# GLA and SSD layer: the attention's gate and V as merged units with tokens on the partitions

## The reference

```python
h = rms_norm(x, pre_norm_w) * (1 + scale) + shift
q, k, v, g, gate_lr, z, xbc, dt_raw = split(h @ w_in)        # GLA head: dk = 128, dv = 256
log_a = log_sigmoid(gate_lr @ gla_gate_w2 + gla_gate_b) / 16
b = cumsum(log_a) in the chunk
q_dec, k_dec, k_end = q * exp(b), k * exp(-b), k * exp(b_last - b)
o = tril(q_dec k_dec^T) v + q_dec S;   S = S * exp(b_last) + k_end^T v
o = rms_norm(o, gla_norm_w)          # over the head's 256 values of a token
o = o * silu(g)
...
out = concat(o, y) @ w_out;  x + gate * rms_norm(out, post_norm_w)
```

## Time and profile before

| what | value |
|---|---|
| median of 3 runs | 1676.37 us (1673.08 to 1678.06) |
| the profiled execution | 1671.3 us, of which span 1669.6 us |
| TensorE busy | 1610.1 us, 96% of the span |
| VectorE / ScalarE / GpSimd busy | 1049.6 / 840.7 / 397.1 us (63% / 50% / 24%) |
| mean granted clock of TensorE | 0.992 of full speed |
| DMA | 231.14 MB, mean 138 GB/s |

### The profile page before, as it was taken

How to read it: one execution, slowest core, us unless ns; L and a number is a source line. 1 busy time by engine, 2 the same in 40 slices (tenths; PEclk the granted TensorE clock), 3 DMA queues, 4 the chain that set the end, 5 groups by cost and what they waited for, 6 DMA issues and landing times. The chain is left out here.

```text
span 1669.6 us, 27425 instructions
## 1 busy us (share of the span) xinstructions
PE 1610.1 (96%) x9990; PEld 1385.7 (83%) x9990; DVE 1049.6 (63%) x1754; ACT 840.7 (50%) x1496; POOL 397.1 (24%) x449
## 2 busy tenths in 40 slices
PE   5999999999999999998999999999999999999997
PEld 4888888888888888888888887888888878888886
DVE  5545454465444554456777777877777754885986
ACT  5755554545544554464454555655455554334332
POOL 2311000101322222200223222223323220451523
PEclk9999999999999999999999999999999999999999
DMA  9523442265434533334222225322212326765886
GB/s 327 139 90 113 143 125 61 83 186 146 159 126 134 188 120 128 124 109 145 74 74 76 73 77 152 113 94 91 77 70 74 113 101 206 244 237 165 314 266 199
DMA packets 131358, 231.14 MB, mean 138 GB/s; under 512 B 9907, under 2 KB 81859, under 8 KB 126134
## 3 DMA queue, kind: packets, MB, share of 16 engines
q1 hardware_dynamic: 123910, 190.76, 35.6%
q10 hardware_dynamic: 6512, 38.80, 6.3%
q0 software_dynamic: 832, 0.22, 0.4%
HBM read 177.05 MB, written 52.70 MB: 138 GB/s over the span
## 5 line engine op out<-in xcount | busy, mean ns | idle before, releaser
L1155 PE MATMUL ps<-hl,w 128*128 128x512 f32 x1488 | 372.9, 399 | 0.1
L1155 PEld LDWEIGHTS ps<-hl,w 128*128 128x128 f32 x1488 | 273.9, 188 | 56.4 <-issue 1.4
L1875 PE MATMUL ps<-hl,w 128*128 128x256 f32 x2304 | 293.6, 287 | 0.0
L1875 PEld LDWEIGHTS ps<-hl,w 128*128 128x128 f32 x2304 | 281.1, 192 | 7.9 <-issue 7.9
L1161 PE MATMUL ps<-w,hl 128*128 128x256 f32 x1536 | 200.6, 287 | 0.0
L1161 PEld LDWEIGHTS ps<-w,hl 128*128 128x128 f32 x1536 | 190.5, 191 | 2.4
L1741 DVE SCALAR_TENSOR_TENSOR c_acc<-c_before,conv_col,c_acc 128x256 f32<-128x256 f32 x288 | 158.3, 551 | 47.2 <-ACT c_acc L1609 40.3
L1879 PE MATMUL ps<-hl 128*128 128x512 f32 x768 | 180.2, 394 | 4.7 <-DVE hl L1710 4.7
L1879 PEld LDWEIGHTS ps<-hl 128*128 128x128 f32 x768 | 144.1, 189 | 34.5 <-DVE hl L1710 4.9
L2264 PE MATMUL ps<-w,hl 128*128 128x512 f32 x720 | 164.4, 390 | 0.0
L2264 PEld LDWEIGHTS ps<-w,hl 128*128 128x128 f32 x720 | 134.9, 188 | 28.6 <-DVE hl L2200 0.4
(11 more groups left out here) (247 smaller groups left out, 2611.8 us busy)
## 6 DMA issues: line engine op xcount, KB each, us to landing
x_sb<-h SPq DMA_DIRECT2D x52, 512.0 KB, 3.9
w_raw<-in_w_in SPq DMA_DIRECT2D x44, 512.0 KB, 5.1
c_ac<-step_sums ACTq DMA_DIRECT2D x16, 1024.0 KB, 4.7
d_a_raw<-mixed_in SPq DMA_DIRECT2D x29, 512.0 KB, 4.1
c_h_raw<-h SPq DMA_DIRECT2D x56, 256.0 KB, 2.8
d_a_raw<-mixed_in SPq DMA_DIRECT2D x11, 1024.0 KB, 5.1
w_sums<-late ACTq DMA_DIRECT2D x8, 1280.0 KB
w_raw<-w_sums SPq DMA_DIRECT2D x40, 256.0 KB, 3.1
```

Of the source, the lines that this page charges most:

```text
L1155: mm = pe.matmul(ps[:, PROJ + u % 2, :], w[:, u, k, a, :], hl[:, par, k, b, :], start=(k == 0 and i == 0), stop=(k == KT - 1 and i == 2))
L1875: mm = pe.matmul(ps[:, PROJ + u % 2, 0:B2], w[:, u, k, a, :], hl[:, par, k, b, :], start=(k == 0 and i == 0), stop=(k == KT - 1 and i == 2))
```

## The change

The gate's two units and V's two become four merged units (u = 2 to 5, `UT` = 2). Merged unit t takes the tile t of 128 tokens as the stationary operand and moves 256 gate columns and 256 V columns at once, twelve matmuls of 512 columns a half; the gate then lies with tokens on the partitions. Step 0 alone, whose later weights arrive one by one, runs gate units and V units of 256 columns. A merged unit is evacuated in two pieces, gate and V.

Gating moves ahead of the turn: VectorE's `gated` computes o_n = o * rstd * SiLU(g) from PSUM in one operation, right behind `update_state` in slot 3t + 1, and waits there for GpSimd's rstd. ScalarE's `normed` keeps the square alone (`square`); behind the turn ScalarE's `weighted` multiplies with the norm's weight and writes `y` (slot 3t + 2). VectorE's `gate_sums` goes ahead of `update_state` in slot 4, `differences` behind the lows; `y_diff` goes to the step's end. `silu_gate` of step n needs all merged units and goes to slot 0 of step n + 1, behind `kt_copy`. A merged unit needs the four blocks 2 to 5, which are in use until the step ends: in a head's last step only blocks 0, 1 and 2 are converted (slots 3, 5, 11), blocks 3, 4, 5 in slots 0, 1, 2 of the next head's first step (`T_SLOTS`). SP loads blocks 4 and 5 at that step's beginning, for the SSD behind the last step. At the end SiLU of step 15 and the conversions of blocks 3, 4 and 5 are spread between the last outputs' operations.

```diff
-    UQ, UK, UG, UV = 0, 1, 2, 4
+    UQ, UK, UT = 0, 1, 2
...
-    W_SLOTS = tuple(2 * u + 3 for u in range(UV))
-    V_SLOTS = (1, 3)
+    W_SLOTS = (3, 5, 3 * TB - 1)
+    T_SLOTS = (0, 1, 2)
...
+        w_t = w[:, UT:U].rearrange("p u k c n -> p (u k c n)").rearrange("p (k c n) -> p k c n", k=KT, c=2)
...
+        gz = sb("gz", [P, 2, TB, DV])
...
+                    if s == 0 and n > 0:
+                        load_w(h, 4)
+                        load_w(h, 5)
...
-                            for u in ((2,), (3, 4), (5,), ())[q]:
+                            for u in ((), (2,), (3,), ())[q]:
...
+                for u in (4, 5):
+                    load_w(GH, u)
...
-                wait(act, unit_done, (h * NB - 1) * U + (u + 1 if u < UV else U))
+                wait(act, unit_done, (h * NB - 1) * U + (u + 1 if u < UT else U))
...
-                elif u in (UG, UG + 1):
-                    wait(act, y_ready, (n - 1) * TB)
-                    dst = gz[:, n % 2, u - UG, :]
+                elif n == 0:
+                    t = (u - UT) % 2 * 2
+                    dst = (gz[:, 0, t:t + 2, :] if u < UT + 2 else v[:, t:t + 2, :]).rearrange("p t n -> p (t n)")
                 else:
-                    wait(act, kv_done, (n - 1) * TB + (u - UV) * 2 + 2)
-                    dst = v[:, (u - UV) * 2:(u - UV) * 2 + 2, :].rearrange("p t n -> p (t n)")
+                    t = u - UT
+                    wait(act, gated_ready, (n - 1) * TB)
+                    act.activation(gz[:, n % 2, t, :], ps[:, PROJ + u % 2, 0:DV], ACT.Copy)
+                    wait(act, kv_done, (n - 1) * TB + t + 1)
+                    act.activation(v[:, t, :], ps[:, PROJ + u % 2, DV:2 * DV], ACT.Copy).then_inc(unit_out, 1)
+                    return
...
-                act.wait_ge(unit_out, n * U + UG + 2)
+                act.wait_ge(unit_out, n * U + U)
                 act.activation(gz[:, n % 2], gz[:, n % 2], ACT.Silu).then_inc(gsilu, 1)
-                act.preload_act_table_set("natural_log_exp_and_others")
+                if n < STEPS - 1:
+                    act.preload_act_table_set("natural_log_exp_and_others")
...
-            def normed(r, t):
+            def square(r, t):
                 m = r * TB + t
                 act.wait_ge(o_done, m + 1)
                 wait(act, mse_ready, m)
                 wait(act, ms_ready, m)
                 act.activation(squares[:, :], ps[:, O, 0:DV], ACT.Square, scale=1.0 / 16.0,
                                accum_out=ms[:, :]).then_inc(ms_ready, 1)
-                act.wait_ge(rstd_ready, m + 1)
-                wait(act, ot_done, m)
-                act.activation(o_n[:, :], ps[:, O, 0:DV], ACT.Copy, scale=rstd[:, :]).then_inc(on_ready, 1)
+
+            def weighted(r, t):
+                m = r * TB + t
+                act.wait_ge(ot_done, m + 1)
+                if r == 0 and t == 0:
+                    act.wait_ge(loads, 96)
+                if t == 0:
+                    wait(act, y_stored, r * 48)
+                for f in range(2):
+                    last = act.activation(y[:, t, f, :], o_turned[:, f * P:(f + 1) * P], ACT.Copy,
+                                          scale=norm_col[:, f:f + 1])
+                last.then_inc(y_ready, 1)
...
+                    if n > 0 and i == 0:
+                        silu_gate(n - 1)
                     if n > 0 and i % 3 == 1:
-                        normed(n - 1, i // 3)
+                        square(n - 1, i // 3)
+                    if n > 0 and i % 3 == 2:
+                        weighted(n - 1, i // 3)
                     if n == 0 and i in (4, 6):
-                        w_high(0, (i - 4) // 2 + UV)
-                    if i in V_SLOTS and s == 0 and n > 0:
-                        w_high(h, UV + V_SLOTS.index(i))
+                        w_high(0, (i - 4) // 2 + 4)
+                    if i in T_SLOTS and s == 0 and n > 0:
+                        w_high(h, 3 + T_SLOTS.index(i))
...
-                    if i == 7:
-                        silu_gate(n)
...
-            for u in range(UV, U):
-                w_high(GH, u)
+            silu_gate(STEPS - 1)
+            w_high(GH, 3)
+            w_high(GH, 4)
...
+            w_high(GH, 5)
+            act.wait_ge(y_stored, (STEPS - 1) * 48)
+            act.wait_ge(ot_done, m + 1)
+            act.activation(y[:, :, 0, :], ps[:, LEFT, :].rearrange("p (t n) -> p t n", n=P), ACT.Copy,
+                           scale=norm_col[:, 0:1]).then_inc(y_ready, 1)
...
-                dve.wait_ge(ot_done, m + 1)
-                if r == 0 and t == 0:
-                    dve.wait_ge(loads, 96)
                 if t == 0:
                     dve.wait_ge(gsilu, r + 1)
-                    wait(dve, y_stored, r * 48)
-                for f in range(2):
-                    last = dve.scalar_tensor_tensor(
-                        out=y[:, t, f, :], in0=o_turned[:, f * P:(f + 1) * P], scalar=norm_col[:, f:f + 1],
-                        in1=gz[:, r % 2, f, t * P:(t + 1) * P], op0=ALU.mult, op1=ALU.mult)
-                last.then_inc(y_ready, 1)
-                if t == TB - 1:
-                    difference(r * TB + TB)
+                dve.wait_ge(rstd_ready, m + 1)
+                wait(dve, ot_done, m)
+                dve.scalar_tensor_tensor(out=o_n[:, :], in0=ps[:, O, 0:DV], scalar=rstd[:, :], in1=gz[:, r % 2, t, :],
+                                         op0=ALU.mult, op1=ALU.mult).then_inc(gated_ready, 1)
...
+                    if i == (6 if n == 0 else 4):
+                        gate_sums(n)
                     if i % 3 == 1 and n > 0:
                         update_state(n - 1, t)
-                    if i % 3 == 2 and n > 0:
                         gated(n - 1, t)
                     if n == 0 and i in (4, 6):
-                        w_low(0, (i - 4) // 2 + UV)
-                    if i == (6 if n == 0 else 4):
-                        gate_sums(n)
-                        differences(n)
-                    if i in V_SLOTS and s == 0 and n > 0:
-                        w_low(h, UV + V_SLOTS.index(i))
+                        w_low(0, (i - 4) // 2 + 4)
+                    if i in T_SLOTS and s == 0 and n > 0:
+                        w_low(h, 3 + T_SLOTS.index(i))
...
+                    if i == (6 if n == 0 else 4):
+                        differences(n)
...
+                if n > 0:
+                    difference(n * TB)
...
+            w_low(GH, 3)
...
+            w_low(GH, 4)
+            dve.wait_ge(gsilu, STEPS)
             dve.wait_ge(xrstd_ready, NB + 1)
-            for t in range(1, TB, 2):
-                dve.tensor_scalar(o_all[:, t, :], ps[:, LAST_O[t], 0:DV], x_rstd[:, t:t + 1], None,
-                                  ALU.mult).then_inc(odd_on_ready, 1)
-            dve.wait_ge(gsilu, STEPS)
+            for t in range(TB):
+                dve.scalar_tensor_tensor(out=o_all[:, t, :], in0=ps[:, LAST_O[t], 0:DV], scalar=x_rstd[:, t:t + 1],
+                                         in1=gz[:, (STEPS - 1) % 2, t, :], op0=ALU.mult,
+                                         op1=ALU.mult).then_inc(gated_ready, 1)
+            w_low(GH, 5)
...
-                    pe.wait_ge(w_ready, h * U + (u + 1 if u < UV else U))
+                    pe.wait_ge(w_ready, h * U + (u + 1 if u < UT else U if n > 0 else (u // 2 + 1) * 2))
...
-                else:
-                    t = (u - UV) * 2 + half
+                elif n == 0:
+                    t, cols = (u - UT) % 2 * 2 + half, slice((u - UT) // 2 * DV, ((u - UT) // 2 + 1) * DV)
                     for k in range(KT):
                         for i, (a, b) in enumerate(PASSES):
                             mm = pe.matmul(ps[:, PROJ + u % 2, half * DV:(half + 1) * DV],
-                                           hl[:, par, k, a, t * P:(t + 1) * P], w_v[:, k, b, :],
+                                           hl[:, par, k, a, t * P:(t + 1) * P], w_t[:, k, b, cols],
+                                           start=(k == 0 and i == 0), stop=(k == KT - 1 and i == 2))
+                else:
+                    t = u - UT
+                    for k in range(half * KT // 2, (half + 1) * KT // 2):
+                        for i, (a, b) in enumerate(PASSES):
+                            mm = pe.matmul(ps[:, PROJ + u % 2, :], hl[:, par, k, a, t * P:(t + 1) * P], w_t[:, k, b, :],
```

38 lines of the change are left out of this document (13 added, 25 removed).

## The result

The changed kernel takes 1681.0 us in the median of 6 runs (1679.9 to 1682.3), beside a median of 1672.7 for six runs of the kernel before (1670.2 to 1678.1): a ratio of 1.0049, 95% interval 1.0037 to 1.0061. The profiled executions stand at 1681.7 (span 1679.9) and 1671.3 (span 1669.6): 10.4 us more. It is slower by 8.4 us in the medians, about half of the 17.3 us by which the forecast of 1690 stands above 1672.7.

A forecast was written before the change was run, and what follows sets the result against it. TensorE bounds the kernel (338 of 345 us busy in the attention's second half). -18.2 + 4.0 + 5.8 + 12.7 + 6.0 + 3.4 = +13.7 us on the profiled 1671.3 gives 1685.0; with 5.1 to the median, 1690, range 1668 to 1702.

The forecast's parts named there:

- Weights at a head: Steps 4, 8, 12: merged unit waits for late weight blocks, 3.5 us each plus 2.2; +12.7 us (8 to 17).
- gains: Wider matmuls 5.6 us, scores' waits for products 7.6, output matmul's waits for masks 5.0; 18.2 us less in sum.
- second rival: Losses at heads, none after the last step or by clock falls, if z's blocks queue less: +4.3 us, 1681; chance 0.13.
- tail: Behind the last step: block conversions end 7.8 us later, 1.8 comes back before z units; +6 us (1 to 9).
- clock: TensorE's clock halves behind long new waits; two of four in steps 4, 8, 11, 12 counted; +3.4 us (0 to 7).
- SiLU in steps 1 to 3: SiLU at the step's head makes the first turn 1.9 us late in steps 1 to 3; +4.0 us (2 to 6).
- scans ahead: Steps 3, 7, 11, 15: scans wait behind a weight block's low part, in 11 meet GpSimd's sums; +5.8 us (3 to 8).
- step 6's products: In step 6 the sums of the gate row stand ahead of VectorE's products, so a scores' wait stays; 1.0 us kept.
- Merged units: Steps 1 to 15: 12 matmuls of 512 columns replace 24 of 256, 6.0 us less; step 0 +0.4; net -5.6.
- masks' gain: Output matmul's seven waits for VectorE's late masks: y products leave the third slot, scans run earlier; 5.0 of 5.2 us gained.

The follow-up runs named there:

- The split: Changed kernel with each merged half unit of steps 1 to 15 run as 24 matmuls of 256 columns instead of 12 of 512; 1.0105 of the kernel before.
- block3_early: Changed kernel with weight block 3 converted earlier in step 0, on ScalarE ahead of evacuations and on VectorE ahead of normalising; 1.0030 of the kernel before.
- silu_after_high: Changed kernel with ScalarE's copy of the turned keys and SiLU ahead of the code's first pass in steps 1 to 3; 1.0032 of the kernel before.
- silu_mask: silu_after_high with VectorE's mask of the first scores also moved ahead of the code's sum in the same slot; 1.0009 of the kernel before.

## Why the prediction was right and where it was not

The direction was right, and the range held the time; the size was about double, 17.3 us forecast above the median of 1672.7 and 8.4 measured. Three things make up the 9 us between. The sum was 3.3 too high on the scale of the profiled execution: +13.7 forecast, +10.4 came. The step from that execution to the median was 3.7 too high: I added 5.1, from three runs of the kernel before with a median of 1676.4; the six runs beside the changed kernel give 1.4, and later series of 30, 23, 11 and 7 runs 1.5 to 3.7. The last 2.0 is which executions happened to be profiled. The step to the median should have been carried as a ratio, and its scatter of 5 us in the range.

Within the sum the step that failed is "Weights at a head": 12.7 us forecast, 7.2 measured, because the load of block 5 was priced at 5.1 us and took 3.9 where it had the DMA to itself. Step 0, put at its matmuls alone, cost 6.05; the gains were 5.2 larger than forecast. The second rival's 1681 is the time that came, but by chance: its condition was no loss at the tail or by the clock, and the tail lost 5.5 and the clock fell.

| term | predicted, us | measured, us |
|---|---|---|
| gains | -18.2 | -23.4 |
| SiLU in steps 1 to 3 | +4.0 | +5.5 (2.16 + 1.68 + 1.68) |
| scans ahead | +5.8 | +3.7 (0.55 + 2.62 + 0.55) |
| weights at heads | +12.7 | +7.2 (3 x 0.66 + 1.18 + 1.57 + 2.48) |
| step 6's products | in the gains | +0.7 |
| tail | +6.0 | +5.5 |
| clock | +3.4 | +5.1, three falls at 1.7 (3.8 against runs without them) |
| block 3 in step 0 | not named | +6.05 in this execution, its clock's fall in it (4.5 to 6.2 with the later runs) |

**Gains.** Merged units: from start to start the 96 V matmuls took 12.01 us of a plain step before, and half of the merged ones take 11.53 after, so 15 x 0.48 = 7.2, less the 0.4 that I count for step 0; forecast 5.6. The split gives 12.8 / 1440 = 8.9 ns for each matmul more, where the rows gave 8.3. The formula of the Trainium skill ("TensorE: Matmul & The Clock Gate", Back-to-back issue gap) for an isolated matmul would make it 2.5, by an estimate; the trace does not agree. A plain step is 40.72, forecast 40.8. Of the 5.2 us that came beyond the forecast, 3.2 are in steps 1 and 2, where waits for x of the kernel before (1.57 and 1.54, twice 0.39) fell to one of 0.68; I had named this and booked it against SiLU, whose net is then 2.3, near the low end of 2 to 6. (In step 1 the clock's fall hides a second wait of 0.68: block3_early, where the clock stayed up there, has one in both steps.) The masks' gain came in full. At tile 2, half of it, the run with the scans behind shows that it was the scans' place and not the y products; at tile 3 it shows that it was not the scans' place, and the y products stay unproven.

**SiLU, scans, tail.** Steps 1 to 3 and the scans of steps 3 and 15 (0.9 forecast, 0.55 came) went as written. In step 11 scans and sums overlapped, 3.44 us instead of the 4.45 that I had taken from step 12, and the wait is 2.62 instead of 4.0. The tail's size was right and its chain only half: it runs through the blocks' places and, for z's third block, through the y stores ahead in SP's queue (its place is free at 768.34, its load issued at 770.76), which I had as the condition of the second rival alone.

**Heads, the step that failed most in size.** The heads lost 1.8, 2.2 and 3.1 us where 3.5, 4.2 and 5.0 were forecast. The chain was right up to the load: block 3's low part ends at 250.90, S + 9.45, forecast S + 9.5. The load behind it I took at 5.1, the median of the earlier trace rows; in step 4 it is converted 3.9 us after its issue (250.92 to 254.82), in step 12 5.2. The median holds loads that share the DMA, as I had written myself, and I used it for one that doesn't: in those 3.9 us the DMA moved 0.52 MB, this load alone. That is 1.2 of the 1.7 us of step 4; the rest is TensorE's, which came to the merged unit at S + 14.6 instead of 14.2. The price added for the store in step 12 was about right (1.5 forecast, 1.3 more than in step 4), and it went when the store was moved; of the 0.7 added in step 8, 0.4 came.

**Clock.** I had priced four waits of 2.8 to 4.3 us at one fall in two. The waits were shorter, three falls came, and one more in step 0. The Trainium skill (the same page, HAM oscillation) tells of a kernel in which every wait for the next operand cost one; this trace agrees with it in part: falls stand behind waits of 2.16, 2.48, 2.62 and 6.2 us, none behind those of 1.18 to 2.05. A fall also cost less than the 1.7 that I took: against runs with the same wait and the clock up it is 0.7 in step 1 (51.31 and 50.61 in block3_early, where TensorE waits for x instead), 1.5 in step 11 and 1.6 in step 12, so 3.8, and the gain is then nearer 22.1 than 23.4.

**What was missing.** I costed step 0 as matmuls alone (+0.4) and didn't ask which weight blocks its first gate unit now waits for. The condition stood in the diff: two blocks for each pair of units instead of one for each. With it the terms would have come out near +20, so the forecast's closeness on the profile's scale is luck: the missing wait made the forecast 6 us too low, the heads and the gains together made it 10.7 too high, and smaller errors went both ways.

## What to carry to other kernels

When operands are regrouped, list for every unit, the first and the last ones above all, which pieces it now needs at once and where each stands in its engine's list; that list of due times, and not the matmuls' durations, decided this change. A new order that wins in the plain step can be kept and its losses mended one operation at a time: here nine moves turned +0.5% into -1.0%. A price for one transfer is taken from a transfer in the same company, and not from the median of all.

## What the runs showed of the hardware

The same wait lets the clock fall in one execution and not in the next: behind the merged unit's wait in step 12 it fell with 2.48, 2.62, 2.19 and 2.17 us and stayed up with 2.44, 2.37, 2.33, 2.31, 2.21 and 2.17. A fall cost 1.6 us there (the period of step 12 is 44.7 with it, 43.1 without), and 3.1 in block3_early, where the clock stood at 0.50 for 6.8 us instead of 3.4. Behind the last outputs' wait of 2.05 us it stayed up in the changed kernel, silu_after_high and silu_mask, and fell in the other five runs that have that wait. I did not find what decides it.

VectorE's four scans take 1.37 us alone and 3.4 to 4.45 beside GpSimd's sums; with the scans moved ahead it was the two differences that ran beside the sums, 1.37 and 1.78 us instead of 0.68, with nobody waiting for them. Who starts first matters: a low part that began 0.05 us ahead of a sum took 1.23 us and the sum 2.33; one that began 0.09 us behind a sum took 2.29, and that sum 1.29.
